# A decoder layer with a table lookup: the first tile's choice computed earlier, eight gathered rows in borrowed memory, the query weights loaded in column halves

## The reference, cut to what matters

```python
q  = (h @ w_q).reshape(tokens, 8, 2, 128)              # h = rms_norm(x), 1024 -> 2048
s1 = einsum('thd,hnd->thn', q[:, :, 0], keys1)         # 8 heads x 128 keys
s2 = einsum('thd,hnd->thn', q[:, :, 1], keys2)
v1, i1 = top_k(s1, 16);  v2, i2 = top_k(s2, 16)
top_score, pos = top_k(all 256 sums v1 + v2, 16)       # 16 experts per head
expert_id = i1 * 128 + i2 at pos;  gate = softmax(top_score)
act = gelu(einsum('tkd,td->tk', u_tab[expert_id], h))  # 128 rows of 1024 per token
x   = x + einsum('tk,tkd->td', gate * act, v_tab[expert_id])
```

## Time and profile before

| what | us |
|---|---|
| median of 3 runs | 1699.85 (1697.36 to 1704.01) |
| the profiled execution, its own time | 1697.94 |
| its span in the trace | 1696.2 |
| first gather issued | 258.56 |
| last v gather issued | 1677.6 |

### The profile page before, as it was taken

How to read it: one execution, slowest core, us unless ns; L and a number is a source line. 1 busy time by engine, 2 the same in 40 slices (tenths; PEclk the granted TensorE clock), 3 DMA queues, 4 the chain that set the end, 5 groups by cost and what they waited for, 6 DMA issues and landing times.

```text
span 1696.2 us, 18239 instructions
## 1 busy us (share of the span) xinstructions
PE 1288.3 (76%) x5996; PEld 660.9 (39%) x5996; DVE 1088.3 (64%) x2840; ACT 249.7 (15%) x480; POOL 985.0 (58%) x1067
## 2 busy tenths in 40 slices
PE   7999899888789887875859756665887656666567
PEld 6899568854456555641316210100440001010111
DVE  4624258967777888877664676667657766666430
ACT  3321421212243321011001010000100000000000
POOL 3000006665776556575557777677777777777774
PEclk9999899998999998787979888888986677677889
DMA  4222608999999999899999999999999999999997
GB/s 151 77 99 88 273 26 282 362 412 410 409 408 405 411 404 382 318 404 413 398 413 409 408 409 409 404 409 384 410 405 409 409 406 406 403 406 406 407 393 304
DMA packets 160847, 599.52 MB, mean 353 GB/s; under 512 B 19312, under 2 KB 19312, under 8 KB 155120
## 3 DMA queue, kind: packets, MB, share of 16 engines
q0 software_dynamic: 147456, 536.94, 80.3%
q1 hardware_dynamic: 13296, 61.42, 9.3%
HBM read 596.18 MB, written 2.10 MB: 353 GB/s over the span
## 4 chain that ended last, share of the span: by engine, by line
DMA 33%; PE 24%; POOL 16%; DVE 15%; issue 8%; DVEq 2%; ACT 1%; SPq 0%; ACTq 0%; POOLq 0%
DMA arena<-in_peer_v,arena 23%; DMA arena<-in_peer_u,arena 10%; POOL arena L600 9%; POOL arena L586 8%; DVE arena L1508 7%; PE psum L895 6%; PE psum L639 4%; PE psum L637 3%; PE psum L857 2%; PE psum L841 2%; PE psum L757 1%; PE psum L750 1%; DVE arena L1200 1%; DVE arena L1414 1%; PE psum L740 1%
## 5 line engine op out<-in xcount | busy, mean ns | idle before, releaser
L895 PE MATMUL psum<-arena 128*32 128x512 f32 x2048 | 635.5, 786 | 328.0 <-DMA arena<-in_peer_v,arena 324.2
L1508 DVE CUSTOM_DVE_ANT_0 arena<-arena,psum 128x1024 f32<-128x1024 f32 x512 | 618.6, 1216 | 322.3 <-DMA arena<-in_peer_u,arena 315.1
L586 POOL DMA_INDIRECT arena<-in_peer_u,arena x512 | 484.9, 947 | 421.3 <-PE psum L841 241.0
L600 POOL DMA_INDIRECT arena<-in_peer_v,arena x512 | 483.1, 944 | 269.5 <-PE psum L895 137.4
L895 PEld LDWEIGHTS psum<-arena 128*32 128x32 f32 x2048 | 102.9, 124 | 808.0 <-DMA arena<-in_peer_v,arena 658.5
L857 PEld LDWEIGHTS psum<-arena 128*128 128x128 f32 x1024 | 115.8, 192 | 10.1 <-issue 10.1
L857 PE MATMUL psum<-arena 128*128 128x128 f32 x1024 | 118.0, 276 | 1.6 <-ACT arena L1082 1.6
L639 PE MATMUL psum<-arena 128*128 128x256 f32 x512 | 118.0, 386 | 0.0
L639 PEld LDWEIGHTS psum<-arena 128*128 128x128 f32 x512 | 96.5, 193 | 20.5 <-issue 8.0
L637 PE MATMUL psum<-arena 128*128 128x256 f32 x384 | 89.3, 390 | 0.8 <-DVE st L1242 0.8
L637 PEld LDWEIGHTS psum<-arena 128*128 128x128 f32 x384 | 73.7, 195 | 16.1 <-issue 4.9
(11 more groups left out here) (216 smaller groups left out, 1176.6 us busy)
## 6 DMA issues: line engine op xcount, KB each, us to landing
arena<-in_w_in SPq DMA_DIRECT2D x28, 1024.0 KB, 7.5
arena<-in_peer_w_q SPq DMA_DIRECT2D x16, 1024.0 KB, 14.8
arena<-in_w_out SPq DMA_DIRECT2D x16, 512.0 KB, 7.2
arena<-in_peer_u,arena POOLq DMA_INDIRECT x512, 10.7
arena<-in_peer_v,arena POOLq DMA_INDIRECT x512, 10.6
arena<-in_x SPq DMA_DIRECT2D x4, 512.0 KB, 4.0
out<-arena SPq DMA_DIRECT2D x32, 64.0 KB, 5.2
arena<-in_norm_g SPq DMA_DIRECT2D x1, 512.0 KB, 18.2
```

The lines of the kernel that those rows point to most:

```text
L586: pool.indirect_dma_start(u_row[n % UB], None, u_d, bass.IndirectOffsetOnAxis(ap=eid[i % 2][:, c:c + 1], axis=0)).then_inc(u_in[n % UB], 16)
L600: pool.indirect_dma_start(row, None, v_d, bass.IndirectOffsetOnAxis(ap=eidT[k % (2 * PH // UH)][:, at_:at_ + 1], axis=0)).then_inc(landed, 16)
L895: mm = pe.matmul(bank[6 + half][group * UK:(group + 1) * UK], zrows[k % 2][:, z0:z0 + ZW], row[:, half * 512:(half + 1) * 512], start=Fals ...
L1508: dve.tensor_tensor_reduce(u_row[n % UB], u_row[n % UB], h2p, 1.0, 0.0, ALU.mult, ALU.add, dots[:, c:c + 1]).then_inc(s["u_free"], 1)
```

## The change

- In BEFORE tile 0's way to its first choice comes first: wo 0, add, n2, h2T, q part 0, s part 0 and the choice stand ahead of most of tile 1's attention. "os" is split: "os" is the output and the new step "st" the state's update, later. The VectorE's "on" for tiles 0 and 1 normalises DeltaNet and attention outputs in one go (12 columns in one rsqrt instead of 4 and then 8).
- VectorE's state update, adds and n2 of tile 1 (HELD) are taken out of its BEFORE and run after dot 7.
- u places 0 to 7 land in eight borrowed places (attention buffers and others), so that they can start before w_out is read: place 0 waits for ("o", 1, 3) and the first choice, 5 for on_rdy, 6 for mix 1, and 8 (the first in the old buffers) for ("wo", 1, 1).
- w_q comes in two column halves of 8 loads each; q parts 0 and 1 need only the first. keysT has memory of its own and is loaded right behind w_q. Tile 1's q and s parts 0 and 1 stand at the end of BEFORE; tile 0's part 3 and tile 1's parts 2 and 3 move into the loop (places 35 to 45).
- v places 0 to 7 are issued with u places 26 to 33 instead of 36 to 43, once ("q", 1, 1) has freed the first half's memory.
- Head 2 is chosen at place 8 instead of 16. The second group: SCALE_AT 26 to 38, BEGIN 34 to 46, DELTA 140 to 146.

```diff
-enumerate([0, 1, 16] + [35 + CHOOSE_EVERY * h ...
+enumerate([0, 1, 8] + [35 + CHOOSE_EVERY * h ...
 # first_group()
+    out += [("z", 0, 0), ("z", 0, 1), ("nw", 0, 0), ("sp", 0, 0), ("r", 0, 0), ("vn", 0, 0), ("sp", 0, 1), ("r", 0, 1),
+            ("o", 0, 0), ("os", 0, 0), ("o", 0, 1), ("osn", 0, 0), ("on", 0, 0), ("nw", 1, 0), ("st", 0, 0),
+            ("z", 1, 0), ("z", 1, 1), ("sp", 1, 0), ("sp", 1, 1), ("mix", 0, 0), ("mix", 0, 1), ("r", 1, 0),
+            ("wo", 0, 0), ("add", 0, 0), ("wo", 0, 1), ("add", 0, 1), ("n2", 0, 0), ("vn", 1, 0), ("z", 1, 2),
+            ("os", 1, 0), ("st", 1, 0), ("h2T", 0, 0), ("h2T", 0, 1), ("r", 1, 1), ("sp", 1, 2), ("z", 1, 3), ("q", 0, 0),
+            ("sp", 1, 3), ("s", 0, 0), ("choose", 0, 0), ("o", 1, 0), ("o", 1, 1), ("r", 1, 2), ("o", 1, 2),
+            ("r", 1, 3), ("o", 1, 3), ("osn", 1, 0), ("on", 1, 0)]
+    out += [("q", 0, 1), ("s", 0, 1), ("mix", 1, 0), ("mix", 1, 1), ("wo", 1, 0), ("wo", 1, 1), ("add", 1, 0), ("add", 1, 1),
+            ("n2", 1, 0), ("xsq", 1, 0), ("q", 0, 2), ("s", 0, 2)]
+    return out + [("h2T", 1, 0), ("h2T", 1, 1), ("q", 1, 0), ("s", 1, 0), ("q", 1, 1), ("s", 1, 1)]
+HELD = {("st", 1, 0): 7, ("add", 1, 0): 7, ("add", 1, 1): 7, ("n2", 1, 0): 7}
+LAST_QUERIES = {35: ("q", 0, 3), 37: ("s", 0, 3), 39: ("q", 1, 2), 41: ("s", 1, 2), 43: ("q", 1, 3), 45: ("s", 1, 3)}
-SCALE_AT, BEGIN = 26, 34
-DELTA = 140
+SCALE_AT, BEGIN = 38, 46
+DELTA = 146
...
+        first_row = [at(k, D) for k in (122, 126, 174, 80, 84, 170, 178, 182)]
+        EARLY, EARLY_AT = 8, 26
 # SyncE
-            for c in range(DC):
-                sp.dma_start(w_q_s[0][c], w_q_d[:, c]).then_inc(s["wq_in"], 16)
+            for half in range(2):
+                for c in range(DC):
+                    sp.dma_start(w_q_h[half][c], w_q_d[:, c, half * NS // 2 * HALF:(half + 1) * NS // 2 * HALF]).then_inc(s["wq_in"], 16)
+            sp.dma_start(keysT, keys_t[0].rearrange("a d n -> d a n")).then_inc(s["keys_in"], 16)
 # gather_u
-                if n >= UB:
+                if n == 0:
+                    pool.wait_ge(*filled("o", 1, SBH // AT_ONCE[1] - 1))
+                elif n == 3:
+                    pool.wait_ge(*filled("st", 1))
+                elif n == 5:
+                    pool.wait_ge(s["on_rdy"], 2)
+                elif n == 6:
+                    for half in range(2):
+                        pool.wait_ge(*filled("mix", 1, half))
+                elif n == FIRST:
+                    pool.wait_ge(*filled("wo", 1, 1))
+                if n >= FIRST + UB:
                     pool.wait_ge(s["u_free"], n - UB + 1)
 # GpSimd's loop
-            pool.wait_ge(*filled("wo", 1, 1))
...
-                if n == LAG:
-                    pool.wait_ge(*filled("q", 1, 3))
-                if n >= LAG:
+                if n == EARLY_AT:
+                    pool.wait_ge(*filled("q", 1, 1))
+                if EARLY_AT <= n < EARLY_AT + EARLY:
+                    gather_v(*divmod(n - EARLY_AT, UK))
+                if n >= LAG + EARLY:
                     gather_v(*divmod(n - LAG, UK))
 # ScalarE: attention logarithms of the first group wait for r of two steps before
+                    if n >= 2 and g == 0:
+                        act.wait_ge(s["r_ps"], n - 1)
 # VectorE: the loop
+                for step in HELD:
+                    if HELD[step] == n:
+                        step_(*step)
```

More of the change, by code:

```diff
@@ L71 @@
 CHOSEN = {(i - 1) * SEL + CHOOSE_AT + CHOOSE_EVERY * h: (i, h) for i in range(1, NT) for h in range(PH)}
-CHOSEN.update({n: (0, h) for h, n in enumerate([0, 1, 16] + [35 + CHOOSE_EVERY * h for h in range(PH - 3)])})
+CHOSEN.update({n: (0, h) for h, n in enumerate([0, 1, 8] + [35 + CHOOSE_EVERY * h for h in range(PH - 3)])})
 PARTS = 6
@@ L210, in places @@
     steps = second_group()
+    for n, step in LAST_QUERIES.items():
+        at.setdefault(n, []).append(step)
     at.setdefault(SCALE_AT, []).append(("xsc", 1, 0))
@@ L240, in banks_of @@
         return [3 if t < GT else 0]
-    if kind in ("mix", "wo") and t < GT:
+    if kind == "wo" and t < GT:
         return [(a, b)[i]]
+    if t == 0 and (kind == "h2T" or kind in ("q", "s") and i == 0):
+        return [(a, b)[i if kind == "h2T" else "qs".index(kind)]]
     if kind in ("h2T", "q", "s"):
@@ L366, in layer_kernel @@
         qs = [at(110, NS, P), at(122, NS, P)]
-        h2T = at(118, DC, P)
+        h2T = [at(k, DC, P) for k in (118, 182, 118, 118)]
         iota = sb("iota", [P, TOPK], U32)
@@ L393, in layer_kernel @@
         v_in = [sem(f"v_in{i}") for i in range(VB)]
+        first_in = [sem(f"first_in{i}") for i in range(FIRST)]
         tail_in = [sem(f"tail_in{i}") for i in range(UB)]
@@ L784, in delta @@
                 elif kind == "os":
[L785 removed]
+                    a = claim("os", t)
                     pe.wait_ge(*read("vn", t))
@@ L1079, in step_ @@
                     act.wait_ge(*filled("h2T", t, i))
-                    if t and i == 0:
+                    if t == 1 and i == 0:
+                        act.wait_ge(s["u_free"], FIRST)
+                    elif t and i == 0:
                         act.wait_ge(*filled("q", t - 1, 3))
-                    act.copy(h2T[:, 4 * i:4 * i + 4], heads(bank_for("h2T", t, i))).then_inc(read("h2T", t, i)[0], 1)
+                    act.copy(h2T[t][:, 4 * i:4 * i + 4], heads(bank_for("h2T", t, i))).then_inc(read("h2T", t, i)[0], 1)
                 elif kind == "q":
@@ L1336, in delta @@
                     dve.drain()
-                    dve.tensor_tensor(S, S, heads(bank_for("os", t, 0, 1)), ALU.add).then_inc(read("os", t, 0, 1)[0], 1)
+                    dve.tensor_tensor(S, S, heads(bank_for("st", t)), ALU.add).then_inc(read("st", t)[0], 1)
                     dve.drain()
@@ L1391, in step_ @@
                     attention(t, i)
-                elif kind == "osn":
+                elif kind == "osn" and t >= GT:
                     dve.wait_ge(s["osq_rdy"], t + 1)
@@ L1506, in _ @@
                     dve.wait_ge(s["h2p_rdy"], i + 1)
[L1507 to L1509 removed]
+                row, landed, times = u_place(n)
+                dve.wait_ge(landed, 16 * times)
+                dve.tensor_tensor_reduce(row, row, h2p, 1.0, 0.0, ALU.mult, ALU.add, dots[:, c:c + 1]).then_inc(s["u_free"], 1)
                 if c % UK == UK - 1:
```

93 lines of the change are left out of this document (53 added, 40 removed), and 4 rows, old and new, of the table out.

## The result

| | before | after |
|---|---|---|
| median of 20 runs, us | 1697.51 (1694.21 to 1704.01) | 1706.33 (1699.5 to 1712.17) |
| profiled execution, us | 1697.94 | 1702.63 |
| its span, us | 1696.2 | 1700.9 |
| ratio of the times | | 1.0045 [1.0035, 1.0056] |

The changed kernel is slower, by 0.45% or 7.6 us (the two medians, over all chips, differ by 8.8; the ratio compares on the same chip). The forecast was 5 us faster. 1706.3 lies inside its range, but the sign is wrong, and that the upper end of the range (1707) reaches it is luck: it was put there for another cause (rival B).

A forecast was written before the change was run, and what follows sets the result against it. A stream of 1024 gathers at 409 GB/s was taken to set the end. Of 10.2 us won by earlier gathers 5.1 remain, with second group and tail at 0: 1699.85 becomes 1695, range 1683 to 1707.

The forecast's parts named there:

- rival B: Slower: the denser second group on places 46 to 146 loses 13.4 us of stream, giving 1708; chance 0.12.
- Part 1: Way to the first gather, tile 0's choice ahead: first gather at 241 instead of 258.6.
- Part 2: First eight rows, then a gap: place 8 at 264, dot 8 at 275.2, 8 us earlier than before.
- Part 3: v rows from place 26: u 26 and v 0 at 298, 45 gathers out instead of 37, 10.2 us ahead.
- Part 4: Stretch from 318 to 352 gives part of the lead back: four gathers remain, 5.1 us.
- Part 5: Second group on 100 places instead of 106: taken as 0, with -6 and +13 as ends.
- Part 6: The tail, the last 36 v rows: as it was, 0.
- A: Rival, the lead is kept: 1689.6, or 1683 with half the dip at 620 saved too; chance 0.28.
- What would show it: Expected trace signs, such as place 8 about 264, dot 8 near 275, w_in from 338, 352 to 620 at 409.

The follow-up runs named there:

- experiment 1: Changed kernel with tile 1's state update in its old place, not held until after dot 7: 1691.84 us, ratio 0.9972 to the kernel before.
- experiment 5: Changed kernel, state update still held, but half 1 of tile 1's wo writes another PSUM bank: 1696.55 us, ratio 0.9996 to the kernel before.
- experiment 4: experiment 1 with the first eight v rows issued late again, with u places 36 to 43: 1693.43 us, ratio 0.9975 to the kernel before.
- experiment 11: experiment 7 with the first eight v rows late again, at places 36 to 43: 1687.81 us, ratio 0.9945 to the kernel before.
- experiment 7: experiment 3 with DELTA 146 instead of 140, second group's first part on 112 places: 1686.43 us, ratio 0.9926 to the kernel before.
- experiment 9: Kernel before with only DELTA changed, 140 to 146: 1692.8 us, ratio 0.9968 to the kernel before.
- experiment 3: Changed kernel with the edits of experiment 1 and experiment 2 together: 1693.86 us, ratio 0.9973 to the kernel before.
- experiment 2: Changed kernel, state update held, last queries back before the loop, second group on its old places (26, 34, 140): 1702.45 us, ratio 1.0027 to the kernel before.
- experiment 6: experiment 1 with place 0 waiting for tile 1's wo again, so no early rows: 1721.61 us, ratio 1.014 to the kernel before.
- experiment 8: experiment 7 with tile 1's mix and wo ahead of tile 0's q and s part 1: 1695.9 us, ratio 0.9988 to the kernel before.
- experiment 10: experiment 7 with head 2 chosen at place 16 again instead of 8: 1690.78 us, ratio 0.9956 to the kernel before.
- experiment 12: experiment 7 with SCALE_AT, BEGIN at 38, 46 instead of 26, 34: 1875.77 us for 1847.4, ratio 1.0137 to the kernel before.

## Why the prediction was wrong, point by point

**Part 1, the first gather at 241: right, 2.2 us late.** 243.18. Choice and first gather came in the order and with the durations that were taken from the earlier trace rows. The choice between full clock (210.5) and low clock (213.4) for wo 0 went to a value between; the second came true: r of tile 1 has its slow pair again, 2.07 us at 195.22, and the second half of wo 0 ended at 213.2. The rule of the Trainium skill that was weighed there (TensorE: Matmul & The Clock Gate, Part 1) agrees as far as the clock halves after idle time. That short breaks would keep the high level, which I read into it, does not hold here: TensorE was idle three times, for 1.17, 1.03 and 1.33 us, and the granted clock from 190 to 200 was 0.69. One more count was off without a price: the issue of the 16 half loads of w_q took SyncE 13.3 us for the 3.9 of the eight loads before, 9.4 more and not 4.

**Part 2, place 8 at 264: this step failed.** The prediction put it as "Place 8 waits for wo 1: q and s part 1 stand ahead of it on TensorE (to 248), mix to 250, wo 13.9: 264", and went on that "It isn't GpSimd that ends the gap". That looked at what stands ahead of wo on TensorE, and not at what its result is written into. Half 1 of the wo needs bank 7, and the reader of that bank had just been put behind dot 7. So the dots came first, then the state update, then the wo, then the add: 269.4 + 8.6 = 278.0, not 264. Both chains hung on that wo, and the last wait before dot 8 was for its row, by 1.07 us (1.11 in experiment 1), not for the VectorE's own steps. What was counted as two chains beside each other, TensorE's to place 8 and the VectorE's to dot 8, was one chain through both: dot 8 at 285.6 instead of 275.2. Experiment 5 shows that the bank is the reason, experiment 1 that with it gone 268.30 and 275.75 come out. The 4 us between 264 and 268.3 are the later start (2.2 us) and the way to wo: mix and then wo wait for ScalarE (0.98 of idle before wo), so that wo began at 254.06 instead of 250.

**Part 3, v from 26: the size was right, the base was off.** With the delay of part 2 u 26 came at 308.03 for 298 and v 0 at 309.27. In experiment 1, where the delay is gone, u 26 is at 298.1 and u 36 at 320.4 with eight v, as counted (298 and 320.2). But nothing of the lead of 10.2 us is seen in the total: experiment 4 without the early v is as fast (0.9975 for 0.9972), and experiment 11 is unclear.

**Part 4, four gathers remain, 5.1 us: nearly right where the state update is early.** Experiment 1's ledger from 241 to 352 is 12.7 + 10.8 + 1.3 + 3.0 = 27.8, so 3.5 us are won against before's 31.3, for 5.1. u 42 was at 327.9 (327), u 44 at 332.5 (334), w_in at 343.92 (338 to 341). In the changed kernel the same term is -6.1 and w_in starts at 354. One wait in it wasn't seen either: ScalarE walks the places too, and its copy of q part 3 at place 35 stands behind the activation of place 32, which waits for dot 31. This is why s part 3 on TensorE shows 16.77 us of idle time at 330.95, with no other engine named. ScalarE's timeline of the changed kernel:

```profile
328.72 0.23 ACT L1177 ACTIVATE arena<-arena 128x32 f32<-128x32 f32 x1 [19.64 <-DVEq L1576]
330.26 0.59 ACT L1139 COPY arena<-psum 128x512 f32<-128x512 f32 x1
```

**Part 5, the second group, 0 with ends of -6 and +13: the net is near 0 in the changed kernel, and it isn't zero in its parts.** The ledgers by the same rule:

| kernel | places of the second group's first part | 241 to 352 | 352 to 620 | 620 to 730 | net | span |
|---|---|---|---|---|---|---|
| after | 46 to 146 | -6.1 | -5.2 | +6.7 | -4.6 | +4.7 |
| experiment 1 | 46 to 146 | +3.5 | -9.2 | +11.8 | +6.1 | -6.2 |
| experiment 7 | 34 to 146 | +4.2 | -2.0 | +10.2 | +12.4 | -11.4 |
| experiment 9 | 34 to 146 | -0.8 | -3.9 | +10.5 | +5.7 | -4.1 |

With DELTA at 146 the stretch from 620 to 730 is fuller in most runs: 398 in experiment 9 with the head of the kernel before, 397 in experiment 7, 403 in experiment 1, against 359 and 377 (experiment 3) with 140. The prediction had this as an end of its range ("if the six places by which the inverse moves against the choices (which stay where they are) suit it better") and no way to see it. But the changed kernel has 384 with 146, near the 381 of experiment 2 with 140. Who waits for whom between 620 and 730, after:

```profile
POOL arena L639 <- PE psum L940: 16.9, 5, 9.3
```

and in experiment 7:

```profile
POOL arena L640 <- PE psum L941: 7.5, 3, 3.2
```

against 15.4 us in four waits. The changed kernel waits the longest there and yet has more bytes than the kernel before, so the sum of these waits doesn't give the rate.

B's loss is there too, 9.2 us in experiment 1 and 5.2 in the changed kernel, between 352 and 620. Most of it lies from 550 to 620 (379 GB/s in the changed kernel, 365 in experiment 1, 386 in experiment 9, 408 in experiment 7, 411 before), right ahead of the old dip, and the border at 620 cuts through what may be one loss. Taken as one stretch the runs fall into three groups:

| inverse at place | places of the second group's first part | runs | GB/s from 500 to 740 |
|---|---|---|---|
| 140 | 106 | before, experiments 2, 3 | 386, 391, 391 |
| 146 | 100 | after, experiments 1, 4, 5, 6 | 388, 390, 388, 389, 391 |
| 146 | 112 | experiments 7, 8, 9, 10, 11 | 397, 403, 396, 398, 401 |

On 100 places the later inverse brings nothing that this stretch shows; on 112 places it brings 5 to 15 GB/s. So the gain of experiments 7 and 9 may be the later inverse, with the denser group taking it back on 100 places, or it may be the greater number of places alone. The run meant to separate these (12) told nothing, and no run has the inverse at 146 on 106 places. It stays open.

**Part 6, the tail: nothing** was seen there. The ledgers close to within 2 us without it, and from 740 to 1640 the stream has 406 GB/s before, after and in experiments 1, 7 and 9. The prediction's "after 730 there is nothing to gain" is too strong for the kernel before (its last 40 us alone lack some 11), but the change doesn't touch it.

**The rivals.** A was nearest to what the change can give (experiment 7, 1686.4, is in its 1683 to 1689.6), but by more bytes between 500 and 740, not by the lead kept. B had the right sign; its loss was there in part (5.2 us, with 6.7 won behind it), but what decided was the wait in part 2, which no rival named. "The changed wait is worse than counted, because a bank's reader was deferred" should have been the one on the other side. By experiments 1 and 5 its price is 8 to 12 us.

**What would show it.** The list in the prediction found the fault at its second entry: the hole before place 8 was 22 us, not 10 to 14. What hangs on it missed as well: dot 8 at 285.6 for 275, v 0 at 309.3 for 299, the stretch to 320 at 321 GB/s for 409, w_in at 354 for 338 to 342. 352 to 620 was at 401 for 409, which was the sign of B.

## What to carry to other kernels

When an engine's step is deferred, look up what it reads, who writes that memory next, and what stands behind that writer: a PSUM bank is a queue like any other, and an order written out by hand doesn't show it. Then keep a ledger of bytes missing against the full stream, stretch by stretch, since terms of 5 to 12 us can cancel in the total, and choose its borders so that none cuts through a dip. (The bank and DELTA could be had one at a time, and were worth 0.5% to 0.7% and 0.3% to 0.5%.) And measure a size that only shifts one group of steps against another (DELTA) on its own; its sign couldn't be read from the busy shares here. Look too whether it changes a second thing, as DELTA does.

## What the runs showed of the hardware

- **One deferred bank costs more than its wait.** TensorE's pause was 8.09 us, then the half took 8.56 us instead of 6.9 (13.97 less 7.11), at a granted clock of 0.89 in that stretch. In experiment 2 it was a pause of 8.08 and then 9.65 us. The Trainium skill (Perfetto Trace Analysis, Optimizing Tensor Performance, Matmuls) advises that independent matmul groups rotate through different PSUM banks, so that one's evacuation overlaps the next; the runs agree in that another bank took the pause away, 8.3 us for the one line of experiment 5.
- **Moving work off TensorE can slow it.** In experiment 8, after 5.77 us of idle, four mix matmuls took 1.08 us for 0.60, and then 13.97 us of matmuls took 16.65, at 0.79 granted for 1.00: part of them ran at the lower of its two levels, 1.2 GHz instead of 2.4.
- **One chip of the study had a slower stream.** The traces of all other runs have 393 to 410 GB/s from 352 to 500. On one chip the same kernel before took 1847 us for 1698, and experiment 12's stream had 358 from 730 to 1690. Nothing in the kernels accounts for it.
- **The start varies by itself, and with it the granted clock.** With the same steps up to the first choice, the first gather went out between 243.0 and 243.9 in eight profiled executions (after; experiments 1, 3, 4, 5, 7, 10, 12) and at 245.96 (experiment 2), 246.6 (experiment 8) and 247.7 (experiment 11) in three. From 20 to 50 us the granted clock was 1.00 in each of the eight and 0.89, 0.87 and 0.89 in the three. The kernel before shows the same pair: 258.56 at 1.00, and 260.87 at 0.89 in experiment 9. What sets it is not shown. It may be a part of why a profiled execution lies off its median: the three late ones are 1.7 to 2.9 us above theirs, while the changed kernel's, an early one, is 3.7 below, which is where 4.7 us in the profiled pair for 7.6 by the ratio may come from. Only the profiled executions have a trace, so the runs don't show it.
